# Head of a two-layer decoder kernel: first weight chunk in larger transfers and by quarters, first stick-breaking chain ahead of two weight splits, one pair of scores a part later

## The reference, cut to what matters

```python
def reference(x, ...):
    h = x
    for i in range(2):
        m = dsa_stick_mixer(h, ...) if i == 0 else moba_mixer(h, ...)
        h = layer_norm(DEEPNORM_ALPHA * h + m, ...)
        h = layer_norm(DEEPNORM_ALPHA * h + swiglu(h, ...), ...)
    return h

def dsa_stick_mixer(x, w_in, kv_norm, w_uk, w_uv, w_out):
    q_a, c_kv, q_idx, k_idx, w_idx, q_b, k_b, v_b = jnp.split(x @ w_in, cuts, axis=-1)
    o_a = dsa_attention(...)             # 8 heads; an indexer picks 64 keys for each query
    o_b = stick_breaking_attention(...)  # 8 heads
    return concat(o_a, o_b) @ w_out

# stick-breaking, strictly causal
z = q . k * HEAD_DIM ** -0.5
log_rem = cumsum(log_sigmoid(-z), reverse) - log_sigmoid(-z)
a = exp(log_sigmoid(z) + log_rem)
```

## Time and profile before

| | |
|---|---|
| time, median of 3 runs | 618.19 us (618.13 to 618.28) |
| time of the profiled execution | 618.07 us |
| its span | 616.3 us |
| PE busy | 603.6 us, 98% |
| DVE, ACT, POOL busy | 412.9, 339.6, 25.9 us |
| DMA | 109.48 MB, mean 178 GB/s |
| mean granted clock | 0.998 |

### The profile page before, as it was taken

The page is one execution under the profiler, slowest core; times in us unless marked ns, Lnnn a source line. Parts: engine busy times, 40 slices in busy tenths (PEclk is TensorE's granted clock), DMA queues, the critical chain, the costliest instruction groups (busy, mean ns, idle before and its releaser), DMA issues.

```text
span 616.3 us, 10303 instructions
## 1 busy us (share of the span) xinstructions
PE 603.6 (98%) x3729; PEld 527.5 (86%) x3729; DVE 412.9 (67%) x668; ACT 339.6 (55%) x631; POOL 25.9 (4%) x49
## 2 busy tenths in 40 slices
PE   7999999999999999999999999999999999999995
PEld 6988887798888888888899999878988888888884
DVE  4698746677756655665886676667776556666546
ACT  5776767265654554455556666653655544555430
POOL 0102012020000000000020000002000000000000
PEclk9999999999999999999999999999999999999999
DMA  8876434446755565555438434451775665556401
GB/s 270 271 237 242 137 103 135 173 148 223 244 176 185 186 204 187 183 187 192 138 115 278 162 130 138 136 209 66 263 231 191 204 203 183 184 181 202 137 1 68
DMA packets 31203, 109.48 MB, mean 178 GB/s; under 512 B 3440, under 2 KB 4464, under 8 KB 31040
## 3 DMA queue, kind: packets, MB, share of 16 engines
q1 hardware_dynamic: 29600, 102.77, 50.2%
q0 software_dynamic: 1568, 6.23, 2.9%
HBM read 107.94 MB, written 1.05 MB: 177 GB/s over the span
## 4 chain that ended last, share of the span: by engine, by line
PE 91%; DMA 3%; DVE 2%; ACT 2%; SPq 1%; issue 1%; DVEq 0%; POOL 0%
PE bank L976 27%; PE bank L892 24%; PE bank L954 12%; PE bank L895 12%; DMA raw<-stream_in 3%; PE bank L906 3%; PE bank L933 2%; PE bank L885 2%; PE bank L1025 2%; PE bank L1036 1%; PE bank L1016 1%; DVE wlo L605 1%; PE bank L939 1%; PE bank L1223 1%; ACT whi L334 1%
## 5 line engine op out<-in xcount | busy, mean ns | idle before, releaser
L605 DVE TENSOR_TENSOR wlo<-raw,whi 128x1024 fp32r<-128x1024 f32 x190 | 226.5, 1221 | 68.1 <-ACT whi L334 67.9
L334 ACT CAST whi<-raw 128x1024 fp32r<-128x1024 f32 x190 | 192.5, 1049 | 22.7 <-DMA raw<-stream_in 22.4
L892 PE MATMUL bank<-hTs,whi 128*128 128x512 f32 x640 | 160.1, 392 | 0.0
L892 PEld LDWEIGHTS bank<-hTs,whi 128*128 128x128 f32 x640 | 116.1, 189 | 21.4
L976 PE MATMUL bank<-whi,oThi 128*128 128x512 f32 x240 | 94.9, 395 | 0.0
L976 PE MATMUL bank<-whi,oTlo 128*128 128x512 f32 x240 | 93.7, 390 | 0.0
L976 PE MATMUL bank<-wlo,oThi 128*128 128x512 f32 x240 | 93.5, 390 | 0.0
L895 PEld LDWEIGHTS bank<-hTs,wlo 128*128 128x128 f32 x640 | 87.3, 190 | 6.3
L895 PE MATMUL bank<-hTs,wlo 128*128 128x256 f32 x640 | 89.2, 282 | 0.0
L954 PE MATMUL bank<-hTs,whi 128*128 128x256 f32 x320 | 60.6, 289 | 0.0
L976 PEld LDWEIGHTS bank<-whi,oThi 128*128 128x128 f32 x240 | 45.1, 188 | 10.0 <-issue 1.5
(11 more groups left out here) (153 smaller groups left out, 701.5 us busy)
## 6 DMA issues: line engine op xcount, KB each, us to landing
raw<-stream_in SPq DMA_DIRECT2D x190, 512.0 KB, 4.5
qT<-ln_rows_in POOLq DMA_DIRECT2D x8, 512.0 KB, 5.1
v<-xT_in SPq DMA_DIRECT2D x4, 256.0 KB, 4.8
kT<-stream_in SPq DMA_DIRECT2D x4, 256.0 KB, 5.0
h<-x_in POOLq DMA_DIRECT2D x1, 1024.0 KB, 7.2
out<-h SPq DMA_DIRECT2D x4, 256.0 KB, 2.0
dist<-consts_in POOLq DMA_DIRECT2D x1, 384.0 KB, 3.6
ukv<-w_uk_in POOLq DMA_DIRECT2D x1, 256.0 KB, 5.6
```

The source lines that it names most:

```text
L334: nc.scalar.copy(whi[:, c % RING, j * HW:(j + 1) * HW], raw[:, c % RAW, j * HW:(j + 1) * HW]).then_inc(whi_ready, 1)
L605: nc.vector.tensor_tensor(wlo[:, c % RING, cols], raw[:, c % RAW, cols], whi[:, c % RING, cols].bitcast(F32), ALU.subtract).then_inc(wlo_r ...
L892: mm(dst[:], whi[:, slot, off + k * P:off + (k + 1) * P], hTs[:, k].rearrange("p j s -> p (j s)"), start=(k == 0), stop=False)
```

## The change

Four edits, all in layer 0's mixer.

1. SP loads chunk 0 in two pieces of 512 KB, one ahead of and one behind two 512 KB pieces of x transposed. ACT and DVE still convert it in four pieces, now column quarters, so that quarters 0 and 1 hold the first output tile. PE does the first output tile over all of x, then the second.
2. ACT splits half 0 of chunk 2 before it evacuates chunk 0's product. PE does the second half of chunk 2 ahead of the four transposes of w_uk.
3. ACT and DVE split chunks 6 and 7 in slot 0 behind the first stick-breaking chain, where they stood ahead of it.
4. In slot 10 the third pair of DSA scores stands behind the slot's first part, and DVE splits its half ahead of these scores' logits.

```diff
@@ sync @@
-            for b in range(4):
-                cols = slice(b * S, (b + 1) * S)
-                sp.dma_start(hT[:, 2 * b:2 * b + 2], xT[:, 2 * b:2 * b + 2]).then_inc(xT_loaded[b], 16)
-                sp.dma_start(first[:, :, cols], stream[0].rearrange("p (j c) -> p j c", j=2)[:, :, cols]
-                             ).then_inc(first_loaded[b], 16)
+            sp.dma_start(first[:, FIRST[0]], stream[0][:, FIRST[0]]).then_inc(first_loaded[0], 16)
+            for j in range(2):
+                sp.dma_start(hT[:, 4 * j:4 * j + 4], xT[:, 4 * j:4 * j + 4]).then_inc(xT_loaded[j], 16)
+            sp.dma_start(first[:, FIRST[1]], stream[0][:, FIRST[1]]).then_inc(first_loaded[1], 16)
@@ scalar @@
+            def first_quarter(i):
+                act.wait_ge(first_loaded[i // 2], 16)
+                nc.scalar.copy(whi[:, 0, QUARTER[i]], first[:, QUARTER[i]]).then_inc(first_hi, 1)
+            first_quarter(0)
+            first_quarter(1)
             for b in range(4):
-                act.wait_ge(xT_loaded[b], 16)
+                act.wait_ge(xT_loaded[b // 2], 16)
                 nc.scalar.copy(hThi[:, 2 * b:2 * b + 2], hT[:, 2 * b:2 * b + 2]).then_inc(hThi_ready, 1)
-                act.wait_ge(first_loaded[b], 16)
-                nc.scalar.copy(first_hi_at[:, :, cols], first[:, :, cols]).then_inc(first_hi, 1)
+            first_quarter(2)
+            first_quarter(3)
             split_hi(1)
+            split_hi_half(2, 0)
             act.wait_ge(chunk_used, 1)
...
-            split_hi(2)
+            split_hi_half(2, 1)
...
-            split_hi(6)
             evac_proj(3, 3, kT[:, 0:2, :])
...
-            split_hi(7)
...
                         nc.scalar.activation(e, e, ACT.Ln, bias=1.0).then_inc(l_ready, 1)
+                if s == 0:
+                    split_hi(6)
+                    split_hi(7)
                 if s != Z_LATE:
                     fill_split_hi(8 + s // 2, s % 2)
@@ vector: the first chunk in the order quarter 0, hTlo 0, quarter 1, hTlo 1 to 3, quarters 2 and 3 @@
-            split_lo(6)
             topk_round(3)
...
-            split_lo(7)
             topk_round(4)
...
+                if s == S_LATE:
+                    split_lo_half(8 + s // 2, s % 2)
                 if s in S_AT:
                     for n in (2 * S_AT[s], 2 * S_AT[s] + 1):
                         logits(n, 2.0 ** (-8.0 * (n + 1) / A_HEADS), dsel[:])
-                split_lo_half(8 + s // 2, s % 2)
+                if s and s != S_LATE:
+                    split_lo_half(8 + s // 2, s % 2)
...
+                if s == 0:
+                    split_lo(6)
+                    split_lo(7)
+                    split_lo_half(8, 0)
                 if s < 3:
                     topk_round(5 + s)
@@ tensor @@
-            for b in range(KT // 2):
-                for j, (w, a) in enumerate(HT_PASSES):
+            for tile in range(2):
+                for b in range(KT // 2):
+                    for j, (w, a) in enumerate(((whi, hThi), (wlo, hThi), (whi, hTlo))):
+                        if j == 0:
+                            pe.wait_ge(hThi_ready, b + 1)
+                            pe.wait_ge(first_hi, 2 * tile + b // 2 + 1)
+                        elif j == 1:
+                            pe.wait_ge(first_lo, 2 * tile + b // 2 + 1)
+                        else:
+                            pe.wait_ge(hTlo_ready, b + 1)
...
             for i in range(I_HEADS):
                 dots(i)
+            proj_half(2, 2, 1, False)
             pe.wait_ge(widx_ready, 1)
             pe.wait_ge(par_loaded, 48)
...
-            proj_half(2, 2, 1, False)
             proj_half(3, 3, 0, False)
...
+                if s == S_LATE:
+                    fill_l0(*FILL0[s], 0)
                 if s in S_AT:
...
-                fill_l0(*FILL0[s], 0)
+                if s != S_LATE:
+                    fill_l0(*FILL0[s], 0)
```

More of the change, by code:

```diff
@@ L108, in build @@
         crawT = dsel[:, 0:S]
-        first = kT[:].rearrange("p (j k) s -> p j (k s)", j=2)
-        first_hi_at = whi[:, 0].rearrange("p (j c) -> p j c", j=2)
-        first_lo_at = wlo[:, 0].rearrange("p (j c) -> p j c", j=2)
+        first = kT[:].rearrange("p k s -> p (k s)")
+        FIRST = [slice(i * CW // 2, (i + 1) * CW // 2) for i in range(2)]
+        QUARTER = [slice(i * CW // 4, (i + 1) * CW // 4) for i in range(4)]
         craw = bank[7][:, 0:S].rearrange("p (t c) -> p t c", t=2)
@@ L132, in build @@
         raw_loaded = [[sem(f"raw_loaded{i}{j}") for j in range(2)] for i in range(RAW)]
-        xT_loaded = [sem(f"xT_loaded{i}") for i in range(4)]
-        first_loaded = [sem(f"first_loaded{i}") for i in range(4)]
+        xT_loaded = [sem(f"xT_loaded{i}") for i in range(2)]
+        first_loaded = [sem(f"first_loaded{i}") for i in range(2)]
         first_hi, first_lo = sem("first_hi"), sem("first_lo")
@@ L179, in build @@
         S_AT, T_AT, AV_AT = {5: 0, 7: 1, 10: 2, 12: 3}, {7: 0, 9: 1, 12: 2, 14: 3}, {8: 0, 10: 1, 13: 2, 15: 3}
-        Z_LATE = 8
+        Z_LATE, S_LATE = 8, 10
         SLOTS1 = 22
@@ L694, in norm, with first_quarter @@
                 split_lo(NORM_CHUNK[n] + AHEAD)
+            def first_quarter(i):
+                dve.wait_ge(first_hi, i + 1)
+                nc.vector.tensor_tensor(wlo[:, 0, QUARTER[i]], first[:, QUARTER[i]],
+                                        whi[:, 0, QUARTER[i]].bitcast(F32), ALU.subtract).then_inc(first_lo, 1)
+            first_quarter(0)
             for b in range(4):
-                cols = slice(b * S, (b + 1) * S)
                 dve.wait_ge(hThi_ready, b + 1)
@@ L701, in _ @@
                                         hThi[:, 2 * b:2 * b + 2].bitcast(F32), ALU.subtract).then_inc(hTlo_ready, 1)
-                dve.wait_ge(first_hi, b + 1)
-                nc.vector.tensor_tensor(first_lo_at[:, :, cols], first[:, :, cols],
-                                        first_hi_at[:, :, cols].bitcast(F32), ALU.subtract).then_inc(first_lo, 1)
+                if b == 0:
+                    first_quarter(1)
+            first_quarter(2)
+            first_quarter(3)
             for c in range(1, AHEAD):
@@ L1054, in _ @@
                 mm(bank[j % 4][:], zeros[:, 0:P], zeros[:], start=True, stop=True)
-            for b in range(KT // 2):
-                for j, (w, a) in enumerate(HT_PASSES):
[L1058 to L1066, removed]
+            for tile in range(2):
[8 more added lines that the diff above has]
+                            pe.wait_ge(hTlo_ready, b + 1)
+                        for k in (2 * b, 2 * b + 1):
                             last = mm(bank[4][:, tile * S:(tile + 1) * S],
                                       w[:, 0, (tile * KT + k) * P:(tile * KT + k + 1) * P], a[:, k, :],
-                                      start=(k == 0 and j == 0 and tile == 0), stop=(k == KT - 1 and j == 2),
-                                      skip_group_check=True)
+                                      start=(k == 0 and j == 0), stop=(k == KT - 1 and j == 2))
             last.then_inc(chunk_used, 1)
```

## The result

| | before | changed |
|---|---|---|
| median | 618.16 us (618.01 to 618.28) | 623.44 us (623.06 to 623.86) |
| profiled execution, span | 618.07, 616.3 | 623.06, 621.3 |
| PE busy | 603.6 | 605.6 |
| mean granted clock | 0.998 | 0.993 |

The ratio is 1.0083, 95% interval 1.0069 to 1.0097: the change costs 0.83%. The forecast was 623.4 within 618.9 to 625.8.

The account below looks back on a forecast made before the run. PE, busy 98% of the span, was taken to bound the kernel, so only its idle time counts. 618.07 - 1.2 (head) - 0.7 (mask) - 0.45 (slot 10) + 5.6 (stall) + 2.1 (clock) = 623.4 us, range 618.9 to 625.8.

Parts of the forecast that it names:

- Head: Chunk 0 and its loads (edit 1): chunk 1 starts at 13.9 for 15.12, saving 1.2 us.
- Edit 2: Chunk 2's earlier half split and product ahead of the w_uk transposes: costed at nothing, with 0.7 us of cover.
- The mask's wait: Slot 2: edit 3 removes PE's wait for a mask, saving 0.7 us.
- The stall: Second stick scores: PE waits 5.6 us for ACT's Exp of line 499, behind chunk 8's and 9's later-loaded casts.
- The clock: Behind the stall: PE's clock falls to half during the idling, costing 2.1 us, bounds 0 and 2.1.
- Slot 10: Edit 4: removes a 0.7 us wait for chunk 8's evacuation, adds a 0.25 us wait; net -0.45 us.
- the stall without the clock's fall: Rival: same 5.6 us stall at the second stick scores, clock stays up, 621.3 us; chance 0.30.
- quick loads: Rival: chunk 8's, 9's and the head's loads land in 3.6 us, stall 2.8, total 617.4 us; chance 0.13.
- no stall: Rival: ACT gets through chunks 8 and 9 in time, so PE doesn't stall, 615.7 us; chance 0.07.
- a later head: Rival: edit 1's larger pieces make PE wait longer at first, head 0.3 us later, 624.9 us; chance 0.08.

Follow-up runs that it names:

- with chunk 6 ahead: Changed kernel with chunk 6 split ahead of the first z chain, behind the evacuations the first scores need; chunk 7 behind the chain: 618.37 us, ratio 0.9996.
- the fastest version: Changed kernel with chunk 6 split before the first z chain and the two Exp of line 499 before chunk 9's first cast: 615.16 us, ratio 0.9947.
- the Exp ahead of the casts: Changed kernel with ACT's two Exp of line 499 ahead of the casts of chunk 8 and chunk 9's first half: 619.57 us, ratio 1.0002.

## Why the prediction was right, step by step

- **Head (-1.2 forecast).** Right in kind, too small: chunk 1 starts at 13.32, 1.8 sooner. The walk's landings, spaced 1.68 us, were late: chunk 0's second half was being cast at 9.2, and chunk 1's first at 10.5 where I had 11.5. So the first tile ended at 10.4 for 10.75, and the second waited for nothing, since quarter 2's rest was ready at 10.5 for 11.15. The wait ahead of chunk 1 is gone, as forecast. The scores start 2.0 sooner, a little more than the head, since ACT's evacuation no longer held them up. That edit 1 pays only with the splits out of this evacuation's way I had not said; the kernel without edit 3 showed it.
- **Edit 2 (nothing).** No wait of PE stands in its place.
- **The mask's wait (-0.7).** Gone, as forecast.
- **The stall (5.6).** It is 5.76, at the place forecast. Counted from the first scores, chunk 9's half was cast from T + 15.3 (15.4 forecast), and the Exp ended at T + 17.1 (17.3). The loads landed after 6.1, 6.2 and 6.4 for the 5.0, 5.9 and 6.9 I took. The reason I gave for long landings was half right: with x out of the way chunk 8 landed sooner, chunk 9 not. That the end fell where I had it is in part luck: chunk 8's landings, 1.1 and 0.3 us later than I took, kept ACT until 52.3, and chunk 9's, 0.5 us sooner, had come at 52.2, so the two errors stand against each other. The rule of the Trainium skill on queue rows ("DMA: Bandwidth & Descriptors", section on queues, rings and completion order) fits chunk 8's landings here, and the 9.2 us of the half issued beside x with chunk 6 ahead. Without x ahead of it, chunk 9's first half took 6.3 us with the four loads 1.14 us apart, and 4.8 with 2.3 and 3.3 us between them (4.1 and 5.5 in the two executions of the fastest version): the closeness of the four makes it late. That is one execution of each, and why the same load took 6.4 us in one and 7.9 in two others, with x ahead of it, stays open.
- **The clock (2.1).** It fell at about 53 and was back at 59.8, and cost 2.4. Two errors stand against each other: the products at the low level took 5.5 us, not 4.2, but at 0.21 us for 0.12 only 0.44 of that is lost, not half. Keeping PE at work removed it.
- **Slot 10 (-0.45).** 88.94 - 61.56 = 27.38 us from the second pair's sums to the fourth pair's scores before, 93.87 - 66.86 = 27.01 after: -0.37, with the new wait of 0.3 where it was forecast:

```profile
93.87 0.70 PE L1135 MATMUL bank<-qT,kT 64*128 64x256 f32 x4 [0.31 <-ACT ukv L505]
```

Sum by the profiles, to the second pair's scores 54.26 - 51.40 = 2.9, then 2.4, then -0.4: 4.9 for the 5.0 by which the span grew. The mechanism held in every term, but for the reason of the long landings; that the time came out within 0.1 us of the forecast is luck. The head and the first scores gave 0.8 more than forecast, the stall and the clock took 0.5 more, and the changed kernel's four executions lie 0.8 us apart. Of the rivals, the stall without the clock's fall (621.3) is what the kernel with PE kept busy comes near; quick loads, no stall and a later head didn't occur.

## What to carry to other kernels

Moving a long step behind a chain takes its releases along: here DVE's splits of chunks 6 and 7 ran 4.7 and 2.4 us later, and with them the loads that go to the same buffer, and the next urgent work stood in the same in-order queue behind the casts of those loads. Before such a move, write down for each urgent instruction what stands ahead of it on its engine, and when that comes free. Put what PE needs next ahead of what only waits for a load, and give the loads their spacing back: the two together turned a loss of 5.3 us into a gain of 3. And judge edits of one path together: without edit 3 the earlier head brought nothing that could be told, and it brought 2.2 us once nothing behind it waited.

## What the runs showed of the hardware

The granted clock was at 1.2 GHz behind much shorter idling than the row that I had to go by. PE had idled 4 us in the earlier trace rows, and about 4.4 when it fell in the changed kernel; but with the load of x later it fell at 51.2, 2.7 us into the stall, and with chunk 6 ahead at 51.0, 2.4 us into it. With the Exp ahead of the casts it fell 0.2 us after PE had resumed from 3.0 us of idling, and once 1 us after PE had resumed from a wait of 1.84 at the head. The waits of up to 1.23 of the earlier trace rows left no trace. The same kernel differs between executions: with the Exp ahead of the casts, and with chunk 6 ahead, those with the lower mean clock took some 2 us more. So a stall of two or three us is to be priced with a chance of some 1.4 to 2.4 us more; this is an estimate, 0.44 of the 3.2 to 5.5 us of products that ran at 1.2 GHz in these profiles. The Trainium skill's rule ("TensorE: Matmul & The Clock Gate", Part 1), that idling brings the clock down and sustained work brings it back, agrees in kind.

A load of 512 KB issued at the same time in two executions (45.76 and 45.78) landed after 6.4 and 7.9 us. The load of x, 1 MB, took 5.1 us when it was issued ahead of the stream's loads, for 7.2 in the earlier trace rows, and 9.2 when it was issued 0.2 us behind a half of the stream, which took 9.2 as well; in the fastest version it was so in both of its profiled executions (9.1 and 9.2).
